# Seven block products instead of eight: Strassen's identity in the second feed-forward of a hybrid decoder layer

## The chip, the cores and the metric

The kernel runs on one core of a Trainium2 chip. The metric is the device time of one execution in microseconds (us). Engine names are TensorE (PE; PEld is its weight load), VectorE (DVE), ScalarE (ACT), GpSimd (POOL) and SyncE (SP), which issues nearly all DMAs.

## The reference

One decoder layer over 512 prompt tokens and 32 sample tokens (T = 544 columns), model width D = 1024, hidden width FF = 2816, all in float32. The layer is a feed-forward, a token mixer and a second feed-forward; each is followed by a layer norm.

```
yp = post_ln(yp, 0.5 * swiglu(yp, ffb_gate, ffb_up, ffb_down), ln3_g, ln3_b)
swiglu(x, w_gate, w_up, w_down) = (silu(x @ w_gate) * (x @ w_up)) @ w_down
post_ln(x, sub, g, b)           = layer_norm(ALPHA * x + sub, g, b)
```

The sample tokens take the same path. Only the second feed-forward (`ffb`) and the norm ahead of it are touched.

## The kernel before

Tokens lie transposed in SBUF: `x[128, 8, 544]`, eight chunks (KC) of 128 model rows. PSUM has eight banks of 512 float32 columns. Every float32 product is made of three products of rounded parts: an operand is split into a high part (ACT copies it to fp32r) and a low part (DVE subtracts the high part from the raw one), and TensorE adds high x high, high x low and low x high. A weight tile of 128 hidden columns is `graw` (raw, 128x1024), `ghi`, `glo`; one buffer of each for gate (0) and up (1).

`product` (L762) makes one gate or up tile: 8 chunks, 3 parts, 2 halves of 272 token columns, so 48 matmuls of 128x128 weights on 272 columns, into banks 0 and 1 (gate) or 2 and 3 (up). There are FT = 22 hidden tiles. They are taken in pairs; the down product of pair p-1 runs between the chunks of pair p:

- `tile(0)` and `tile(1)` (L930) make the first pair. `tile(0)` waits for the norm chunk by chunk (`norm_lo`); between the chunks of `tile(1)` stand five `rows_back` (L915), which transpose the normed tokens back for the residual.
- `window(i, par, p)` (L944) runs ten times. It makes pair p+1, and after every four chunks one `block` (L885) of pair p: 6 matmuls on 512 columns into bank 4, 5 or 6, which DVE adds to `yt` in `add_rows` (L1871). `few` (L904) does the same for the 32 sample tokens.
- A tail makes the down product of the last pair, and `rows_scale` and `rows_values` the last layer norm.

ACT per pair: silu of two gate tiles (`sg`, L1471), high parts of four weight tiles (L1392), of the hidden values (`hh`, L1467) and of the down weights (`ehi`, L1460). DVE per pair: the low parts of these (L1741, `hl` L1895, `elo` L1868), two gated products `ht` (L1890), eight `add_rows` (L1875) and one `add_few` (L1880). GpSimd does nothing in this stage. SP loads `graw` strips of 512 KB and `eraw` strips of 1 MB, each when its buffer is free.

Each engine runs its own program in a fixed order, and waits on semaphores that other engines count up.

The norm ahead (`norm_values(1)`, L1984, on DVE; `norm_scale(1)`, L1550, on ACT): DVE multiplies a chunk by the reciprocal deviation (L2014), ACT makes `xh` and `x` from it (L1565), DVE makes `xl` (L2010).

## Time and profile before

| | |
|---|---|
| median of 3 runs | 1372.5 us (1369.28 to 1373.71) |
| profiled execution, first to last instruction | 1372.2 us |
| PE, DVE, ACT, POOL busy | 94%, 55%, 31%, 18% of the span |
| mean granted TensorE clock | 0.978 |

The times of the three runs are given without saying which execution was profiled; its span of 1372.2 us lies among them, 0.3 us under their median, so the profiled execution can stand for the runs. What lies around the span is not recorded apart. A reader should ask first which engine is busy without a gap in the stage that changes, and only then what its instructions cost.

### The profile page before, as it was taken

The page shows a single profiled execution, that of the slowest core. Times are in us where ns is not written, and L with a number is a line of the kernel's source. Part 1 is how long each engine was busy: PE and PEld are TensorE (multiplying, and loading weights), DVE is VectorE, ACT ScalarE, POOL GpSimd, SP SyncE. Part 2 cuts the span into 40 slices and gives each one's busy share as a digit, 9 for nine tenths or more (in the row PEclk, how much of TensorE's full clock was granted, in tenths as well). Part 3 has the DMA queues.
Part 4 walks back from the last instruction along what each step waited for, and adds up shares of the span by engine and source line. Part 5 has one row for each costly group of instructions (what it writes and reads, how often), then busy time and mean ns, then how long its engine had stood idle before and what let it go on. Part 6 is the DMA issues. An engine that isn't in the chain of part 4 may idle for free.

```text
span 1372.2 us, 29896 instructions
## 1 busy us (share of the span) xinstructions
PE 1293.8 (94%) x11917; PEld 1180.1 (86%) x11917; DVE 756.9 (55%) x1215; ACT 431.1 (31%) x813; POOL 241.1 (18%) x237
## 2 busy tenths in 40 slices
PE   6999999999999888999989999896999999999996
PEld 5999999999999877999956666695999999999994
DVE  4676487467737765334446666647344444344446
ACT  4322222223312225222235555316321222122224
POOL 1352044114404405000135334000000000000000
PEclk9999999999999999999989999898999999999998
DMA  4887176246625522322278665132532333333211
GB/s 140 223 214 178 57 207 194 70 133 182 186 79 171 160 55 63 66 63 78 73 237 263 205 226 170 36 89 80 162 102 85 105 97 102 107 107 102 82 61 65
DMA packets 216192, 173.95 MB, mean 127 GB/s; under 512 B 22947, under 2 KB 206418, under 8 KB 215700
## 3 DMA queue, kind: packets, MB, share of 16 engines
q1 hardware_dynamic: 209940, 155.64, 38.6%
q0 software_dynamic: 6144, 16.79, 3.7%
q8 instruction: 78, 1.28, 0.4%
q14 instruction: 30, 0.25, 0.1%
HBM read 168.44 MB, written 8.10 MB: 129 GB/s over the span
## 4 chain that ended last, share of the span: by engine, by line
PE 78%; DVE 11%; ACT 4%; DMA 3%; issue 3%; SPq 1%; POOL 0%; DVEq 0%; ACTq 0%
PE ps L770 44%; PE ps L899 8%; PE ps L826 7%; PE ps L796 4%; DVE dlo L1746 3%; PE ps L1255 2%; DMA draw<-in_ffa_down_dram 2%; DVE glo L1741 1%; PE ps L1226 1%; PE ps L1291 1%; PE ps L1271 1%; PE ps L1340 1%; PE ps L1003 1%; PE ps L1213 1%; ACT xh L1565 1%
## 5 line engine op out<-in xcount | busy, mean ns | idle before, releaser
L770 PE MATMUL ps<-xh,ghi 128*128 128x272 f32 x1872 | 395.1, 293 | 16.9 <-DVE xl L2010 14.2
L770 PE MATMUL ps<-xl,ghi 128*128 128x272 f32 x1872 | 388.8, 289 | 0.0
L770 PE MATMUL ps<-xh,glo 128*128 128x272 f32 x1872 | 387.4, 288 | 0.0
L770 PEld LDWEIGHTS ps<-xh,ghi 128*128 128x128 f32 x1872 | 299.5, 189 | 33.8 <-issue 17.6
L770 PEld LDWEIGHTS ps<-xl,ghi 128*128 128x128 f32 x1872 | 296.2, 190 | 0.0
L770 PEld LDWEIGHTS ps<-xh,glo 128*128 128x128 f32 x1872 | 295.3, 190 | 0.0
L1741 DVE TENSOR_TENSOR glo<-graw,ghi 128x1024 fp32r<-128x1024 f32 x117 | 144.0, 1231 | 108.0 <-ACT ghi L1392 105.8
L726 POOL COPY perm<-landing 128x1024 f32<-128x1024 f32 x64 | 140.9, 2215 | 304.0 <-DMA landing<-in_cache_cmp_kv_dram 303.9
L1816 DVE SCALAR_TENSOR_TENSOR x<-ps,x 128x544 f32<-128x544 f32 x176 | 126.8, 720 | 104.7 <-PE ps L826 104.3
L1875 DVE SCALAR_TENSOR_TENSOR yt<-ps,yt 128x512 f32<-128x512 f32 x88 | 60.6, 691 | 156.6 <-PE ps L899 156.6
L1392 ACT ACTIVATE ghi<-graw 128x1024 fp32r<-128x1024 f32 x117 | 122.7, 1049 | 30.9 <-PE ps L770 20.9
L1398 ACT ACTIVATE dhi<-draw 128x128 fp32r<-128x128 f32 x176 | 53.2, 307 | 228.2 <-PE ps L826 207.9
L1746 DVE TENSOR_TENSOR dlo<-draw,dhi 128x128 fp32r<-128x128 f32 x176 | 108.1, 614 | 18.5 <-ACT dhi L1398 18.5
L399 POOL DMA_DIRECT2D page<-in_cache_sel_kv_dram x128 | 70.1, 549 | 227.4 <-issue 223.3
L826 PE MATMUL ps<-hh,dhi 128*128 128x272 f32 x352 | 77.2, 301 | 15.7 <-DVE dlo L1746 15.7
L826 PEld LDWEIGHTS ps<-hh,dhi 128*128 128x128 f32 x352 | 55.2, 190 | 21.7 <-DVE dlo L1746 21.1
L826 PE MATMUL ps<-hl,dhi 128*128 128x272 f32 x352 | 73.4, 290 | 0.0
L826 PE MATMUL ps<-hh,dlo 128*128 128x272 f32 x352 | 73.4, 290 | 0.0
L899 PE MATMUL ps<-ehi,hh 128*128 128x512 f32 x176 | 69.9, 397 | 1.7 <-DVE yt L1875 1.1
L899 PE MATMUL ps<-ehi,hl 128*128 128x512 f32 x176 | 69.4, 394 | 0.0
L899 PE MATMUL ps<-elo,hh 128*128 128x512 f32 x176 | 69.4, 394 | 0.0
L1467 ACT ACTIVATE hh<-ht 128x512 fp32r<-128x512 f32 x22 | 13.9, 632 | 159.3 <-DVE ht L1890 159.3
(344 smaller groups left out, 1492.5 us busy)
## 6 DMA issues: line engine op xcount, KB each, us to landing
landing<-in_cache_cmp_kv_dram SPq DMA_DIRECT2D x256, 128.0 KB, 2.5
page<-in_cache_sel_kv_dram SPq DMA_DIRECT2D x128, 128.0 KB, 4.9
page<-in_cache_sel_kv_dram POOLq DMA_DIRECT2D x128, 128.0 KB, 5.0
graw<-in_ffa_gate_dram SPq DMA_DIRECT2D x22, 512.0 KB, 4.9
graw<-in_ffa_up_dram SPq DMA_DIRECT2D x22, 512.0 KB, 4.1
draw<-in_ffa_down_dram SPq DMA_DIRECT2D x88, 128.0 KB, 2.8
graw<-in_w_in_dram SPq DMA_DIRECT2D x44, 256.0 KB, 3.3
graw<-in_ffb_gate_dram SPq DMA_DIRECT2D x22, 512.0 KB, 3.9
```

Of the source, the lines that this page charges most:

```text
L399: eng.dma_start(dst[:, DS(at + (j + k), 1), :], pool[0, DS(page, 1)].rearrange("o p c g d -> p o (c g d)")).then_inc(landed, 16)
L726: pool.tensor_copy(perm[:, :, :, at:at + QUAD].rearrange("p x d a -> p a x d"), landing[j % 2][:].rearrange("p a (x d) -> p a x d", d=HD)) ...
L770: last = nc.tensor.matmul(out[:, h, 0:HALF], a[:, k, :], b[:, k, h * HALF:(h + 1) * HALF], start=(k == 0 and a is hi and b is xhi), stop=( ...
L796: last = nc.tensor.matmul(ps[c * HD:(c + 1) * HD, bank + h, 0:G * PW], w1[rows, c, d, :], perm[rows, c * G:(c + 1) * G, d, :], start=(d == ...
L826: last = nc.tensor.matmul(ps[:, 4 + 2 * s + h, 0:HALF], a[:], b[:, h * HALF:(h + 1) * HALF], start=(a is dhi[s] and b is hh[par]), stop=(a ...
L899: last = nc.tensor.matmul(ps[:, 4 + k, :], x_part[:, rows], w_part[:, a, :], start=(a == 0 and x_part is h and w_part is ehi[n]), stop=(a ...
L1392: act.activation(ghi[s][:], graw[s][:], ACT.Copy).then_inc(w_hi[s], 1)
L1398: act.activation(dhi[s][:], draw[k % 2][:, s, :], ACT.Copy).then_inc(d_hi[s], 1)
L1741: dve.tensor_tensor(glo[s][:], graw[s][:], ghi[s][:].bitcast(F32), ALU.subtract).then_inc(w_lo[s], 1)
L1746: dve.tensor_tensor(dlo[s][:], draw[k % 2][:, s, :], dhi[s][:].bitcast(F32), ALU.subtract).then_inc(d_lo[s], 1)
L1816: dve.scalar_tensor_tensor(xt, ps[:, 4 + 2 * s:6 + 2 * s, 0:HALF], 0.5, xt, ALU.mult, ALU.add).then_inc(y_added[s], 1)
L1875: dve.scalar_tensor_tensor(part, ps[:, 4 + k, :], 0.5, part, ALU.mult, ALU.add).then_inc(y_added[0], 1)
```

## The change

The product of a pair of hidden tiles with the tokens is seen as a 2x2 by 2x2 block product: hidden tiles (2) by upper and lower half of the model width (2), times halves of the width by token halves, `near` (columns 0 to 271) and `far` (272 to 543). It is made from seven block products instead of eight (Winograd's form of Strassen's identity). A block product (`part`) has 4 chunks and 3 split parts, 12 matmuls of 272 columns. Seven left operands per pair and matrix: three blocks of the weights (A11, A12, A22) and four sums (S1 to S4), which GpSimd makes in `sums`. Seven right operands: three blocks of the tokens and four sums t1 to t4 (`tokens_of`), made once, after the norm.

- A group (w, s) is pair w, gate (s = 0) or up (s = 1). There are 11 x 2 groups. The operands of group g+1 are split while group g runs, into seven slots `slot_hi` and `slot_lo`.
- Four results come from seven products: ACT copies three partial sums out of PSUM (`snap`), DVE adds them to others (`quarter`), and further products add onto what stands in the bank.
- SP loads 256 hidden columns at once (1 MB, `pair_w`), and the loops are written out.
- The first two loads, and the stores of the key and value rows, are issued before `std_ready` is waited for.

```diff
+PARTS = 7
+WINDOWS = FT // 2
+A11, A12, S1, S2, S3, S4, A22 = range(PARTS)
+LOW_ORDER = (A11, A12, S1, S3, S2, S4, A22)
+LOW_AT = {k: n + 1 for n, k in enumerate(LOW_ORDER)}
...
+        t1 = (xh[:, upper, far], xl[:, upper, far], x_raw[:, upper, far])
+        tokens_of = ((xh[:, upper, near], xl[:, upper, near]), (xh[:, lower, near], xl[:, lower, near]), t1[0:2],
+                     (t2[0][:], t2[1][:]), (t3[0][:], t3[1][:]), (xh[:, lower, far], xl[:, lower, far]),
+                     (t4[0][:], t4[1][:]))
...
-                def gate_up(s, i):
-                    w = (gate, up)[s]
-                    col = value(i * 128)
-                    free_from(w_lo[s], i + (uses[s] + ONE))
-                    sp.dma_start(graw[s][:], w[0].rearrange("(k p) f -> p k f", p=128)[:, :, DS(col, 128)]
-                                 ).then_inc(dma_w[s], 16)
+                def group_load(s, p):
+                    g = 2 * (p - 1) + s
+                    if p:
+                        sp.wait_ge(*since("slot_low", PARTS * (g + 1)))
+                        sp.wait_ge(*since("s_made", 4 * (g + 1)))
+                    sp.dma_start(pair_w[s][:], (gate, up)[s][0].rearrange("(k p) f -> p k f", p=128)[:, :, p * 256:(p + 1) * 256]
+                                 ).then_inc(q[f"dma_wide{s}"], 16)
...
                 token_stores()
+                sp.wait_ge(stored, 16 * KV_STORES)
...
+            def sums(g):
+                p, s = divmod(g, 2)
+                a = lambda i, j: pair_w[s][:, (upper, lower)[j], i * 128:(i + 1) * 128]
+                at = lambda k: slot_raw[:, k]
+                def free(k):
+                    if g:
+                        pool.wait_ge(*since("part", PARTS * (g - 1) + k + 1))
+                pool.wait_ge(*since(f"dma_wide{s}", 16 * (p + 1)))
+                free(S1)
+                pool.tensor_tensor(at(S1), a(1, 0), a(1, 1), ALU.add).then_inc(q["s_made"], 1)
+                free(S2)
+                pool.wait_ge(*since("s_made", 4 * g + 1))
+                pool.tensor_tensor(at(S2), at(S1), a(0, 0), ALU.subtract).then_inc(q["s_made"], 1)
+                free(S3)
+                pool.tensor_tensor(at(S3), a(0, 0), a(1, 0), ALU.subtract).then_inc(q["s_made"], 1)
+                free(S4)
+                pool.wait_ge(*since("s_made", 4 * g + 2))
+                pool.tensor_tensor(at(S4), a(0, 1), at(S2), ALU.subtract).then_inc(q["s_made"], 1)
+            sums(0)
+            pool.wait_ge(normed, 2 * KC)
+            pool.tensor_tensor(t3[2][:], x[:, lower, far], x[:, upper, far], ALU.subtract
+                               ).then_inc(q["t3_raw"], 1)
+            for g in range(1, 2 * WINDOWS):
+                sums(g)
...
+                def part(g, k, bank, first):
+                    pe.wait_ge(*since("slot_low", PARTS * g + LOW_AT[k]))
+                    bh, bl = tokens_of[k]
+                    for c in range(K2):
+                        for a, b in ((slot_hi, bh), (slot_hi, bl), (slot_lo, bh)):
+                            last = nc.tensor.matmul(ps[:, bank, 0:HALF], a[:, k, c, :], b[:, c, :],
+                                                    start=(first and c == 0 and a is slot_hi and b is bh),
+                                                    stop=(c == K2 - 1 and a is slot_lo), skip_group_check=True)
+                    last.then_inc(q["part"], 1)
+                def group(w, s, between):
+                    g = 2 * w + s
+                    if w:
+                        pe.wait_ge(*since(("silu_done", "up_done")[s], 4 * w))
+                    if g == 0:
+                        pe.wait_ge(norm_lo, KC + K2)
+                    part(g, A11, s, True)
+                    if g:
+                        pe.wait_ge(*since("mixed_out", 3 * g - 2))
+                    else:
+                        pe.wait_ge(norm_lo, 2 * KC)
+                    part(g, A12, 2, True)
+                    between(0)
+                    if g:
+                        pe.wait_ge(*since("mixed_out", 3 * g))
+                    else:
+                        pe.wait_ge(*since("t_low", 1))
+                    part(g, S1, 3, True)
+                    pe.wait_ge(*since("snapped", 3 * g + 1))
+                    if g == 0:
+                        pe.wait_ge(*since("t_low", 2))
+                    part(g, S2, s, False)
+                    between(1)
+                    pe.wait_ge(*since("snapped", 3 * g + 3))
+                    if g == 0:
+                        pe.wait_ge(*since("t_low", 3))
+                    part(g, S3, s, False)
+                    between(2)
+                    part(g, S4, 3, False)
+                    pe.wait_ge(*since("mixed_out", 3 * g + 2))
+                    if g == 0:
+                        pe.wait_ge(*since("t_low", 4))
+                    part(g, A22, s, False)
+                    between(3)
...
+                    def blocks(n):
+                        def between(at):
+                            if n == 0 and at == 1:
+                                if p == 0:
+                                    pe.wait_ge(q["yt_begun"], QT + 1)
+                                few(p, par)
+                            for j in ((), (0,), (1,), (2, 3))[at]:
+                                block(p, par, QT * n + j, row_block)
+                        return between
+                    group(w, 0, blocks(0))
+                    group(w, 1, blocks(1))
...
+            def high(g, k):
+                p, s = divmod(g, 2)
+                if g:
+                    act.wait_ge(*since("part", PARTS * (g - 1) + k + 1))
+                if k in (A11, A12, A22):
+                    act.wait_ge(*since(f"dma_wide{s}", 16 * (p + 1)))
+                else:
+                    act.wait_ge(*since("s_made", 4 * g + k - S1 + 1))
+                act.activation(slot_hi[:, k], raw_block(s, k), ACT.Copy).then_inc(q["slot_high"], 1)
...
+                def silu(w, n, a, cols, src=None):
+                    dst = sg4[2 * (w % 2) + a][:, cols]
+                    if src is None:
+                        act.wait_ge(*since("mixed_out", 6 * w + n + 1))
+                    else:
+                        act.wait_ge(*since("part", PARTS * 2 * w + PARTS))
+                        if w >= 2:
+                            act.wait_ge(*since("h_low", 2 * (w - 1)))
+                    act.activation(dst, dst if src is None else src, ACT.Silu).then_inc(q["silu_done"], 1)
+                def snap(g, n):
+                    act.wait_ge(*since("part", PARTS * g + (1, 3, 4)[n]))
+                    if g:
+                        act.wait_ge(*since("mixed_out", 3 * (g - 1) + (1, 2, 3)[n]))
+                    act.activation((sum1, sum3, sum2)[n][:], ps[:, 3 if n == 1 else g % 2, 0:HALF], ACT.Copy
+                                   ).then_inc(q["snapped"], 1)
+                def group(w, s):
+                    g, p = 2 * w + s, w - 1
+                    more = g + 1 < 2 * WINDOWS
+                    if s == 0 and w:
+                        copy_h(p, 1)
+                    snap(g, 0)
+                        high(g + 1, A11)
+                    if s == 0 and w:
+                        split_e(1, p, p == 0)
+                    if s == 1:
+                        split_e(0, w, w == 0)
+                    if more:
+                        high(g + 1, A12)
+                    if s == 0:
+                        silu(w, 0, 0, near)
+                    if w == 0:
+                        rows_begun(0 if s == 0 else QT)
+                    snap(g, 1)
+                    snap(g, 2)
+                    if more:
+                        high(g + 1, S1)
+                        high(g + 1, S2)
+                    if g == 0:
+                        rows_begun(1)
+                    if s == 0:
+                        silu(w, 1, 1, far)
+                    if g == 0:
+                        rows_begun(2)
+                    if more:
+                        high(g + 1, S3)
+                    if s == 0:
+                        silu(w, 2, 0, far)
+                    if more:
+                        high(g + 1, S4)
+                    if s == 0:
+                        silu(w, 3, 1, near, ps[:, 0, 0:HALF])
+                    else:
+                        copy_h(w, 0)
+                    if g == 0:
+                        rows_begun(3)
+                    if more:
+                        high(g + 1, A22)
...
+                    for k in (A11, A12, S1, S2):
+                        high(0, k)
...
+            def slot_lower(g, k):
+                n = LOW_AT[k] - 1
+                dve.wait_ge(*since("slot_high", PARTS * g + k + 1))
+                if g:
+                    dve.wait_ge(*since("part", PARTS * (g - 1) + k + 1))
+                if k in (S1, S2):
+                    dve.wait_ge(*since("s_made", 4 * g + (2, 4)[k - S1]))
+                dve.tensor_tensor(slot_lo[:, k], raw_block(g % 2, k), slot_hi[:, k].bitcast(F32), ALU.subtract
+                                  ).then_inc(q["slot_low"], 1)
...
+                def quarter(w, s, n, a, cols, out_part, first, second):
+                    g = 2 * w + s
+                    dst = (sg4, ht4)[s][slot_of(w, a)][:, cols]
+                    dve.wait_ge(*since("part", PARTS * g + out_part))
+                    dve.wait_ge(*since("snapped", 3 * g + n + 1))
+                    dve.tensor_tensor(dst, first, second, ALU.add).then_inc(q["mixed_out"], 1)
+                    if s == 1:
+                        dve.wait_ge(*since("silu_done", 4 * w + 4))
+                        dve.wait_ge(*since("mixed_out", 3 * g + n + 1))
+                        last = dve.tensor_tensor(dst, dst, sg4[slot_of(w, a)][:, cols], ALU.mult)
+                        last.then_inc(q["up_done"], 1)
+                        if n == 2:
+                            dve.wait_ge(*since("up_done", 4 * w + 3))
+                            dve.engine_nop().then_inc(q["h_ready"], 1)
...
+                    if s == 0 and w >= 1:
+                        low(p, 1)
                     if more:
-                        split_w(0, i + (uses[0] + 2))
-                    add_rows(p, 6, row_block)
-                    split_e(0, p + 1)
-                split_w(0, uses[0] + 1)
+                        slot_lower(g + 1, A11)
+                    quarter(w, s, 0, 0, near, 2, bank(2), sum1[:])
+                    if more:
+                        slot_lower(g + 1, A12)
+                    if s == 0 and w:
+                        split_e(1, p)
+                    if s == 1:
+                        split_e(0, w)
+                    if w:
+                        if p == 0 and s == 0:
+                            dve.wait_ge(q["yt_begun"], QT + 1)
+                        add_rows(p, 4 * s, row_block)
+                        if s == 0:
+                            add_few(p)
+                    if more:
+                        slot_lower(g + 1, S1)
+                    quarter(w, s, 1, 1, far, 5, bank(s), sum3[:])
+                    if w:
+                        add_rows(p, 4 * s + 1, row_block)
+                    if more:
+                        slot_lower(g + 1, S3)
+                    quarter(w, s, 2, 0, far, 6, bank(3), sum2[:])
+                    if more:
+                        slot_lower(g + 1, S2)
+                    if s == 1:
+                        dve.wait_ge(*since("part", PARTS * g + PARTS))
+                        dve.tensor_tensor(ht4[slot_of(w, 1)][:, near], bank(s), sg4[slot_of(w, 1)][:, near], ALU.mult
+                                          ).then_inc(q["up_done"], 1)
+                        dve.wait_ge(*since("up_done", 4 * w + 4))
+                        dve.engine_nop().then_inc(q["h_ready"], 1)
+                        low(w, 0)
+                        add_rows(p, 4 * s + 2, row_block)
+                    if more:
+                        slot_lower(g + 1, S4)
+                        slot_lower(g + 1, A22)
...
                 low(KC - 2)
                 low(KC - 1)
+                if n == 1:
+                    def token_low(k, dst, src, high_part):
+                        dve.wait_ge(*since("t_high", k + 1))
+                        dve.tensor_tensor(dst, src, high_part.bitcast(F32), ALU.subtract
+                                          ).then_inc(q["t_low"], 1)
+                    raw1, raw2, raw4 = t1[2], t2[2][:], t4[2][:]
+                    dve.tensor_tensor(raw1, x[:, upper, far], x[:, upper, near], ALU.subtract).then_inc(q["t_raw"], 1)
+                    dve.wait_ge(*since("t_raw", 1))
+                    dve.tensor_tensor(raw2, x[:, lower, far], raw1, ALU.subtract).then_inc(q["t_raw"], 1)
+                    token_low(0, t1[1], raw1, t1[0])
+                    slot_lower(0, S3)
+                    dve.wait_ge(*since("t_raw", 2))
+                    dve.tensor_tensor(raw4, x[:, lower, near], raw2, ALU.subtract).then_inc(q["t_raw"], 1)
+                    slot_lower(0, S2)
+                    token_low(1, t2[1][:], t2[2][:], t2[0][:])
+                    token_low(2, t3[1][:], t3[2][:], t3[0][:])
+                    slot_lower(0, S4)
+                    token_low(3, t4[1][:], t4[2][:], t4[0][:])
+                    slot_lower(0, A22)
             ffa_values()
             norm_values(0)
```

## Rows read from the trace of the kernel before

**Rows 1.** The page: engines (busy us, share, instructions); a group (busy us, mean ns).

```profile
PE 1293.8 (94%) x11917; PEld 1180.1 (86%) x11917; DVE 756.9 (55%) x1215; ACT 431.1 (31%) x813; POOL 241.1 (18%) x237
...
L770 PEld LDWEIGHTS ps<-xh,ghi 128*128 128x128 f32 x1872 | 299.5, 189 | 33.8 <-issue 17.6
```

**Rows 2.** Windows: stretch, length, busy us of each engine, PEclk, DMA share, GB/s.

```profile
1032.00:1064.00 32.00, 32.00 (x228) 29.41 (x227) 13.59 (x17) 7.44 (x10) 0.00 (x0) 1.00 0.28 84
...
1192.00:1224.00 32.00, 32.00 (x229) 29.41 (x228) 14.69 (x18) 6.11 (x8) 0.00 (x0) 1.00 0.35 110
```

**Rows 3.** The chain that ended last, 1188 to 1230 us: start, us, what.

```profile
1191.25 3.00 PE ps L770 x24
1194.25 1.40 PE ps L899 x6
...
1227.64 2.39 PE ps L770 x19
```

**Rows 4.** Timeline of PE, eight transposes with eight different weights between products.

```profile
968.81 1.03 PE L923 MATMUL ps<-ident,x 128*128 128x128 f32 x8
969.60 0.50 PE L770 MATMUL ps<-xh,ghi 128*128 128x272 f32 x2
```

**Rows 5.** Groups by form, 960 to 1372 us: busy us, mean ns of one, idle before.

```profile
L1875 DVE SCALAR_TENSOR_TENSOR yt<-ps,yt 128x512 f32<-128x512 f32 x88 | 60.6, 691 | 156.6 <-PE ps L899 156.6
L1741 DVE TENSOR_TENSOR glo<-graw,ghi 128x1024 fp32r<-128x1024 f32 x42 | 51.2, 1218 | 9.0 <-ACT ghi L1392 9.0
...
L1895 DVE TENSOR_TENSOR hl<-ht,hh 128x512 fp32r<-128x512 f32 x22 | 15.0, 683 | 1.4 <-ACT hh L1467 1.4
L1467 ACT ACTIVATE hh<-ht 128x512 fp32r<-128x512 f32 x22 | 13.9, 632 | 159.3 <-DVE ht L1890 159.3
...
L1880 DVE SCALAR_TENSOR_TENSOR ys<-ps,ys 128x256 f32<-128x256 f32 x11 | 4.7, 424 | 17.7 <-PE ps L911 17.7
...
L1487 ACT ACTIVATE ys<-ps 128x256 f32<-128x256 f32 x1 | 0.4, 384 | 1.1 <-PE ps L926 1.1
```

**Rows 6.** Timeline of DVE at the end: two instructions in a row.

```profile
1357.73 1.28 DVE L1875 SCALAR_TENSOR_TENSOR yt<-ps,yt 128x512 f32<-128x512 f32 x2
```

**Rows 7.** Groups of POOL, whole span.

```profile
L726 POOL COPY perm<-landing 128x1024 f32<-128x1024 f32 x64 | 140.9, 2215 | 304.0 <-DMA landing<-in_cache_cmp_kv_dram 303.9
...
L754 POOL TENSOR_TENSOR xl<-yconv,xh 128x544 fp32r<-128x544 f32 x4 | 5.4, 1344 | 0.3
```

**Rows 8.** Timeline, POOL and DVE, 67 to 76 us, while both work.

```profile
67.04 4.03 POOL L726 COPY perm<-landing 128x1024 f32<-128x1024 f32 x2 [8.72 <-DMA landing<-in_cache_cmp_kv_dram]
73.73 3.18 POOL L726 COPY perm<-landing 128x1024 f32<-128x1024 f32 x1 [2.66 <-DMA landing<-in_cache_cmp_kv_dram]
...
69.02 0.71 DVE L1816 SCALAR_TENSOR_TENSOR x<-ps,x 128x544 f32<-128x544 f32 x1
69.66 1.38 DVE L1746 TENSOR_TENSOR dlo<-draw,dhi 128x128 fp32r<-128x128 f32 x1
...
73.75 1.22 DVE L1741 TENSOR_TENSOR glo<-graw,ghi 128x1024 fp32r<-128x1024 f32 x1
```

**Rows 9.** Timeline, DVE in the norm ahead of the stage.

```profile
937.03 1.29 DVE L1995 TENSOR_TENSOR sq<-sq 128x1088 f32<-128x1088 f32 x1 [1.18 <-ACT sq L1555]
...
957.27 0.72 DVE L2010 TENSOR_TENSOR xl<-x,xh 128x544 fp32r<-128x544 f32 x1 [0.74 <-ACT x L1565]
```

**Rows 10.** Timeline, PE at the start of the stage.

```profile
947.89 0.79 PE L770 MATMUL ps<-xh,ghi 128*128 128x272 f32 x2 [5.75 <-DVE xl L2010]
948.48 0.66 PE L770 MATMUL ps<-xl,ghi 128*128 128x272 f32 x2
948.94 0.65 PE L770 MATMUL ps<-xh,glo 128*128 128x272 f32 x2
...
981.25 0.41 PE L770 MATMUL ps<-xh,ghi 128*128 128x272 f32 x2
```

**Rows 11.** Timeline, PE at the end of the last window.

```profile
1345.14 0.40 PE L899 MATMUL ps<-elo,hh 128*128 128x512 f32 x1
1345.47 1.07 PE L911 MATMUL ps<-eraw,ht 128*32 128x256 f32 x16
1346.97 0.47 PE L899 MATMUL ps<-ehi,hh 128*128 128x512 f32 x1 [0.43 <-DVE hl L1895]
```

**Rows 12.** DMA issues: KB each, median us from issue to landing.

```profile
eraw<-in_ffb_down_dram SPq DMA_DIRECT2D x11, 1024.0 KB, 4.9
w<-in_cmp_w_dram SPq DMA_DIRECT2D x4, 1024.0 KB, 8.3
```

More of the change, by code:

```diff
@@ L238, in trunk, with raw_under, split_pair @@
         rows = ExitStack()
-        sb("under_rows", [128, 12000], F32, rows)
+        def raw_under(name, shape):
+            with ExitStack() as over:
+                return sb(name, shape, F32, over)
+        def split_pair(name):
+            upper_part = sb(f"{name}_0", [128, KC // 2, HALF], F32R, rows)
+            raw_part = raw_under(f"{name}_raw", [128, KC // 2, HALF])
+            return upper_part, sb(f"{name}_1", [128, KC // 2, HALF], F32R, rows), raw_part
+        t2 = split_pair("t2")
+        t3 = split_pair("t3")
+        sb("under_groups", [128, T], F32, rows)
+        sum3 = sb("sum3", [128, HALF], F32, rows)
+        sb("before_groups", [128, 896 - T - HALF], F32, rows)
+        pair_w = [sb(f"pair_w{n}", [128, KC, 256], F32, rows) for n in range(2)]
+        slot_hi = sb("slot_hi", [128, 7, KC // 2, 128], F32R, rows)
+        slot_raw = raw_under("slot_raw", [128, 7, KC // 2, 128])
+        slot_lo = sb("slot_lo", [128, 7, KC // 2, 128], F32R, rows)
+        t4 = split_pair("t4")
+        ln_rows = sb("ln_rows", [128, 2, D], F32, rows)
+        ln_s = sb("ln_s", [128, 2, 256], F32, rows)
+        eraw = sb("eraw", [128, 2, D], F32, rows)
         over = ExitStack()
@@ L889, in block @@
                     if j == 0:
-                        pe.wait_ge(hl_ready, p * 2 + (FT + 2 + ONE))
+                        pe.wait_ge(*since("h_low", p * 2 + 2))
                     if order is row_block:
@@ L944, in window @@
-                def window(i, par, p):
-                    def first(c):
-                        if c % 4 == 0:
-                            if c == 4:
-                                pe.wait_ge(q["yt_begun"], QT + 1)
-                            block(p, par, c // 4 - 1, row_block)
-                        if c == 6:
-                            few(p, par)
-                    def second(c):
-                        if c % 4 == 0:
-                            block(p, par, QT + c // 4 - 1, row_block)
-                    tile(i, None, first)
-                    tile(i + 1, None, second)
@@ L961, in ffb_products @@
-                pe.wait_ge(std_ready, 4)
-                tile(0, (norm_lo, KC))
-                turns = {2: 0, 4: 1, 8: 2, 12: 3, 14: 4}
-                tile(1, None, lambda c: rows_back(turns[c]) if c in turns else None)
-                with pe.Fori(0, FT // 4) as i:
-                    for par in range(2):
-                        window(i * 4 + (2 + 2 * par), par, i * 2 + par)
+                def part(g, k, bank, first):
[7 more added lines that the diff above has]
+                    last.then_inc(q["part"], 1)
@@ new lines, in first_gate, with first_up @@
+                def first_gate(at):
+                    rows_back(at)
+                def first_up(at):
+                    if at == 0:
+                        rows_back(QT)
+                group(0, 0, first_gate)
+                group(0, 1, first_up)
+                for w in range(1, WINDOWS):
+                    p, par = w - 1, (w - 1) % 2
+                    def blocks(n):
[9 more added lines that the diff above has]
+                    group(w, 1, blocks(1))
@@ L1525, in rows_scale @@
+                for w in range(WINDOWS):
+                    for s in range(2):
+                        group(w, s)
+                copy_h(WINDOWS - 1, 1)
+                split_e(1, WINDOWS - 1)
             def rows_scale():
@@ L1570, in norm_scale, with token_high @@
                     affine(x[:, k, :], x[:, k, :], k).then_inc(normed, 1)
+                if n == 1:
+                    def token_high(k, dst, src):
+                        if k == 2:
+                            act.wait_ge(*since("t3_raw", 1))
+                        else:
+                            act.wait_ge(*since("t_raw", (1, 2, 0, 3)[k]))
+                        act.activation(dst, src, ACT.Copy).then_inc(q["t_high"], 1)
+                    token_high(0, t1[0], t1[2])
+                    token_high(1, t2[0][:], t2[2][:])
+                    high(0, S3)
+                    token_high(2, t3[0][:], t3[2][:])
+                    high(0, S4)
+                    token_high(3, t4[0][:], t4[2][:])
+                    high(0, A22)
             ffa_gates()
@@ L2009, in low @@
                     dve.wait_ge(normed, KC * n + k + 1)
-                    dve.tensor_tensor(xl[:, k, :], x[:, k, :], xh[:, k, :].bitcast(F32), ALU.subtract
+                    cols = near if n == 1 and k < K2 else slice(0, T)
+                    dve.tensor_tensor(xl[:, k, cols], x[:, k, cols], xh[:, k, cols].bitcast(F32), ALU.subtract
                                       ).then_inc(norm_lo, 1)
```

226 lines of the change are left out of this document (82 added, 144 removed).

## The prediction, made before the changed kernel ran

> **What bounds the kernel now.** I read the page first [rows 1]: TensorE is busy 94% of the span. That is a mean over stages, so I then read the second feed-forward in stretches of 32 us: TensorE is busy in all 32, at full clock (2.4 GHz), VectorE in 14, ScalarE in 6 to 7, GpSimd in none [rows 2]. The chain of work that ended last says the same in order of time: 24 products of 3.00 us, 6 down products of 1.40 us, and again, with nothing between [rows 3]. So here a matmul taken away is time taken away, as long as no other engine comes to hold TensorE up. The same piece stands at 1191.25 and at 1227.64 us: a window lasts 36.39 us. The ten windows begin at 981.25 [rows 10] and end at 1345.14 + 0.23 = 1345.37 (the last down matmul starts at 1345.14 [rows 11]; six take 1.40, so one 0.23), and 1372.2 - 1345.4 = 26.8 us of tail follow.
>
> **TensorE's own work.** A pair had 2 x 2 x 48 = 192 gate and up matmuls and gets 2 x 7 x 12 = 168. At 3.00 us for 24, one costs 0.125 us, so a pair loses 3.0 us and a window becomes 33.4 us; eleven pairs save 33. Before, each load of weights served one of two halves, and now each load brings other weights. Bounded from both sides: the profile has a weight load for every matmul already (11917 of each [rows 1]), and eight transposes with eight different weights start within 0.79 us, 0.10 us apiece [rows 4], under 0.125. So I take 0.125, the nearest row. The other end is 0.19, a weight load's own duration [rows 1], if each load had to end before its matmul and began after the last: windows of 44 us. Already 0.132 would undo the gain, so this is a rival below.
>
> The Trainium skill (TensorE: Matmul & The Clock Gate, "Back-to-back issue gap") gives a sustained 81 ns for 128 columns and 131 ns for 512. An estimate between these is 105 ns for 272 columns, by which 264 matmuls would save 28 us and not 33; the trace has 125 ns and about 232 ns, so the sum goes by the trace.
>
> **VectorE's work in a window.** A following instruction costs less than its own duration: two of 691 ns take 1.28 us [rows 5, 6], so 0.60 to 0.64 us apiece; I take 0.60 for 512 columns, 1.14 for 1024 (1218 less 0.08) and 0.36 for 272 (424 less 0.08 for 256). Low parts of slots 14 x 0.60 = 8.4 (before 4 x 1.14 = 4.6); down weights 2 x 1.14 = 2.3; additions of rows 8 x 0.60 and 0.35 = 5.2; hidden low parts 1.2; quarters 6 additions and 4 products, 10 x 0.36 = 3.6, and some 0.5 of waits for itself: 21.2 us of 33.4. ScalarE: 14 slots, 6 snaps, 4 silus, 2 hidden and 2 down copies, at 0.55, 0.33, 0.33, 0.55 and 0.97 us from its rows [rows 5], are 14 us. Both fit.
>
> **GpSimd's work.** Eight sums of 128x512. The nearest row is a two-operand instruction on 544 columns, 1344 ns [rows 7]: 1.27 us apiece, 10.1 per window. Below it can hardly be less, since the row has contiguous operands and these are strided; from above, the copy of 1024 strided columns takes 2.1 us undisturbed (two in 4.03 [rows 8]), and if two inputs of 512 cost as much as one of 1024, a sum takes 2.1. I take 1.27, the same operation.
>
> **They hold each other up.** While GpSimd copies (67.04 to 71.07), a subtraction of 128x128 on VectorE starting at 69.66 takes 1.38 us, that is until 71.04, where GpSimd ends; the same instruction takes 0.3 elsewhere. The other way round, the copy from 73.73 takes 3.18 us where VectorE subtracts 1024 columns at 73.75. But the addition from PSUM at 69.02 keeps its 0.71 [rows 8]. So VectorE's instructions with both inputs in SBUF and GpSimd's sums exclude one another: 8.4 + 2.3 + 1.2 + 1.1 (three products) = 13.0 and 10.1 us, 23.1 of 33.4. Even if VectorE stood still during every sum it would be 31.4. It fits, with 2 us to spare in the worst case.
>
> The Trainium skill (SBUF — State Buffer, "Who interferes with whom") calls this an exclusive lock held for the whole instruction. The rule alone, which lets either side wait fully, makes 31.4 us in a window the ceiling; the walk below has less. The trace agrees on the exclusion and on the PSUM exception.
>
> **Order within a group.** TensorE waits where a sum is copied out: `S3` waits for the snap after `S2`. Between them stands one down block, 1.40 us; ScalarE needs about 0.2 to notice, 0.35 to copy: 0.8 spare. `A22` waits for the quarter after `S3`: between them a block and `S4`, 2.9 us, and VectorE may be behind a slot's low part which waits for GpSimd's second sum. Walking both groups with these prices, VectorE ends the gate group 1 us late and the up group 2.4 us late, and catches up in the 4 us before the next down block; the quarter is ready 1.7 us early at its tightest. Loads: 1 MB lands in 5 to 8 us [rows 12] and has some 9 in hand. So I cost the steady window at 33.4 and no stall.
>
> **The start is dearer.** Before, tile 0 ran chunk by chunk behind the norm from 947.89, and the windows began at 981.25 [rows 10]. Now the third product waits for token sums. VectorE finishes the norm at 957.27 + 0.72 = 958.0 [rows 9], 0.3 later for two more copies on ScalarE. GpSimd's token sum (1088 columns, 2 x 1.34 = 2.7 us) gets in first: 961. Then VectorE has 3 token subtractions and 4 token low parts, 1.21 apiece (1.29 less 0.08 [rows 9]), four slot low parts, 0.7 of waits, and two sums of GpSimd (2.5) that hold it: about 14 us, 975. Only then come one slot's low part and the first quarter (976), on which ScalarE's silu, one copy of rows back, and the two snaps wait (978.5); `S3` waits for these. What is left of the first pair on TensorE: three products of group 0 and seven of group 1 at 1.5, transposes of 2.3, one uncovered snap of 0.8: 18.1, 996.6. TensorE will have stood still for over 5 us again (its second product and transposes end near 973), and after such a pause its matmuls cost 0.23 instead of 0.125 for some 5 us [rows 10]: 2.3 more, 999. That is 17.7 us later than 981.25. Bounds: 989 if GpSimd never holds VectorE and the clock stays up; 1006 if each hold is twice as long.
>
> The tail is unchanged: the hidden low part is ready about as late after the last block as it was (a wait of 0.43 [rows 11]).
>
> **Sum.** 999 + 10 x 33.4 + 0.3 + 26.8 = 1360.1 us for the span; with 0.3 for what the median lies above it [1372.5 against 1372.2], 1360.4. That is 12 us, 0.9%, faster: 30 saved in the windows, 18 lost at the start. Its own range, by the bounds of the start and half a microsecond per window, is 1350 to 1368.
>
> **The rivals.**
>
> *The start is hidden.* If the silu and snaps don't stand behind the token work, the start costs nothing more: 1372.5 - 33 = 1339, up to 1350 when half of it shows. Against it: the instruction order on VectorE puts all token low parts before the first quarter. 0.06.
>
> *Stalls in the window.* Each group has two waits with 0.8 and 1.7 us to spare; if a group loses 0.6 us, the ten windows are 34.6 us each and the gain is gone: 1372. Half to double of that is 1366 to 1384. For it: a 1.27 us sum is longer than the spare. Against it: in the walk ScalarE needs nothing from VectorE between `S1` and the snap in the up group. 0.15.
>
> *GpSimd bounds the stage (slower).* If a sum takes 2.1 us and VectorE is held for all of each, a window is 21.2 + 8 x 2.1 = 38.0 us: 999 + 380 + 27 = 1406. It decides from (34.6 - 21.2) / 8 = 1.68 us per sum. For it: strided inputs, and VectorE's queue in fixed order, which makes a hold of one instruction a delay of all. Against it: the 1344 ns row, and that additions from PSUM aren't held. 0.13.
>
> *Other weights cost.* At 0.14 us per matmul instead of 0.125 a window is 168 x 0.14 + 12.3 (down products and sample tokens: 36.4 less 24.1) = 35.8 us, the end 999 + 358 + 27 = 1384; at 0.132 nothing is gained. For it: this is the one thing that the trace of before shows only for 128 columns. Against it: there it is 0.10 us [rows 4]. 0.06.
>
> **Chances.** My forecast has 0.60, the four rivals 0.06, 0.15, 0.13 and 0.06. A measurement of this kernel can tell about 0.3% (4 us) from no change. Faster: 0.60 + 0.06 + 0.05 of the stalls + 0.01 of the weights = 0.72. Slower: 0.13 + 0.05 + 0.03 = 0.21. Within: the other 0.07. The range leaves out most of the first rival and of the third: 1346 to 1384.
>
> **What would show it.** Right: the chain in the windows alternates 12 products of 1.5 us with blocks, 33.4 us between equal pieces, TensorE at 32 of 32; POOL's sums near 1.3 us; the first window begins near 999 after a pause of some microseconds before the first `S3`. Wrong: idle time of PE before a part, released by ACT `sum` (snap) or DVE (quarter, slot low part); POOL sums over 1.7 us; VectorE's slot low parts at well over 0.68 us in the mean; products more than 0.125 apart within a part.

## The result, and the profile after

The changed kernel takes 1359.55 us (median of 5, 1355.53 to 1360.82), the kernel before, run beside it, 1369.28 (1364.48 to 1373.71): a ratio of 0.9912 with a 95% interval of 0.9886 to 0.9939, so 0.9% faster. The prediction's sum was 1360.4, its range 1346 to 1384. The profiled execution took 1359.71 us, its span is 1358.1.

The page's first part answers to [rows 1]: TensorE has 264 matmuls fewer and 29 us less to do, VectorE, ScalarE and GpSimd have more.

```profile
PE 1264.8 (93%) x11653; PEld 1150.5 (85%) x11653; DVE 864.7 (64%) x1420; ACT 508.2 (37%) x1015; POOL 375.0 (28%) x326
```

Windows of 33 us in the second feed-forward (columns as in [rows 2]):

```profile
1136.00:1169.00 33.00, 33.00 (x230) 30.11 (x229) 22.76 (x38) 14.73 (x28) 11.85 (x9) 1.00 0.32 108
1237.00:1270.00 33.00, 33.00 (x230) 30.11 (x229) 22.76 (x38) 14.97 (x28) 11.88 (x9) 1.00 0.33 108
```

TensorE is still busy in all of the stretch at full clock. VectorE went from 14 to 23 us, ScalarE from 7 to 15, GpSimd from nothing to 12, and none of it reaches TensorE. The chain that ended last agrees (start, us, what; with [rows 3]):

```profile
1114.62 6.03 PE ps L1024 x48
1124.95 3.03 PE ps L1024 x24
1127.98 2.80 PE ps L987 x12
1130.78 6.02 PE ps L1024 x48
1137.81 1.58 PE ps L987 x6
...
1148.13 6.03 PE ps L1024 x48
```

1148.13 - 1114.62 = 33.51 us is a window, where 36.39 was. 48 matmuls take 6.03: 0.126 us apiece, though the weights now change ahead of two matmuls in three (`part` uses a high weight block for two matmuls in a row, a low one for one), where they changed ahead of one in three. The sample tokens' row comes once per pair and is the easiest clock for windows (PE's timeline):

```profile
1001.34 1.07 PE L999 MATMUL ps<-eraw,ht 128*32 128x256 f32 x16
...
1136.73 1.07 PE L999 MATMUL ps<-eraw,ht 128*32 128x256 f32 x16
```

It stands at 1001.34, 1036.21, 1069.72 and so on to 1304.27: a first window of 34.87 and then 33.51 or 33.50 each time. The first is 1.36 us longer, nearly all of it one wait for the snap of a bank on ScalarE, which no later window has:

```profile
1005.10 0.52 PE L1024 MATMUL ps<-t,slot_hi 128*128 128x272 f32 x2 [1.10 <-ACT sum L1626]
```

ScalarE's snap is queued behind a silu that waits for VectorE's first quarter (L2083), and that quarter is late because two of VectorE's low parts, 0.68 us when free, met GpSimd's sums for the next group:

```profile
1000.17 1.79 DVE L2073 TENSOR_TENSOR hl<-ht,hh 128x512 fp32r<-128x512 f32 x1
1001.88 1.77 DVE L2062 TENSOR_TENSOR slot_lo<-pair_w,slot_hi 128x512 fp32r<-128x512 f32 x1
1003.58 0.43 DVE L2083 TENSOR_TENSOR sg<-ps,sum 128x272 f32<-128x272 f32 x1
...
1000.04 1.37 POOL L829 TENSOR_TENSOR slot_raw<-pair_w 128x512 f32<-128x512 f32 x1 [4.35 <-PE ps L1024]
1001.56 1.55 POOL L832 TENSOR_TENSOR slot_raw<-slot_raw,pair_w 128x512 f32<-128x512 f32 x1
```

**The start.** PE's timeline again: the norm's last product, the waits, and the first row of the second pair.

```profile
931.50 8.78 PE L1124 MATMUL ps<-sq,mean_w 128*128 128x272 f32 x24 [2.06 <-ACT sq L1709]
950.05 0.59 PE L1024 MATMUL ps<-xh,slot_hi 128*128 128x272 f32 x1 [9.77 <-DVE xl L2220]
958.50 0.59 PE L1024 MATMUL ps<-xh,slot_hi 128*128 128x272 f32 x1 [5.35 <-DVE xl L2220]
967.54 0.49 PE L1024 MATMUL ps<-t,slot_hi 128*128 128x272 f32 x2 [3.55 <-DVE t L2232]
975.21 0.82 PE L1024 MATMUL ps<-t,slot_hi 128*128 128x272 f32 x2 [3.56 <-ACT sum L1626]
990.58 0.51 PE L1024 MATMUL ps<-t,slot_hi 128*128 128x272 f32 x2 [0.49 <-ACT sum L1626]
...
995.20 0.29 PE L1024 MATMUL ps<-xh,slot_hi 128*128 128x272 f32 x1
```

Where one long wait of 5.75 us stood [rows 10], TensorE now stands still four times, 22.2 us together. VectorE's and GpSimd's timelines show what is done meanwhile:

```profile
955.41 3.03 DVE L2220 TENSOR_TENSOR xl<-x,xh 128x544 fp32r<-128x544 f32 x1 [0.74 <-ACT x L1721]
958.37 1.28 DVE L2236 TENSOR_TENSOR x_raw<-x 128x1088 f32<-128x1088 f32 x1
...
970.37 1.75 DVE L2062 TENSOR_TENSOR slot_lo<-pair_w,slot_hi 128x512 fp32r<-128x512 f32 x1
...
972.78 0.43 DVE L2083 TENSOR_TENSOR sg<-ps,sum 128x272 f32<-128x272 f32 x1
...
955.39 2.47 POOL L841 TENSOR_TENSOR t_raw<-x 128x1088 f32<-128x1088 f32 x1 [34.14 <-ACT x L1721]
...
970.03 1.54 POOL L832 TENSOR_TENSOR slot_raw<-slot_raw,pair_w 128x512 f32<-128x512 f32 x1 [4.34 <-PE ps L1024]
```

The norm's last low part takes 3.03 us instead of 0.72: it starts 0.02 us after GpSimd's token sum of 2.47, waits for it, and then runs. From 958.37 to 972.78 lie 14.4 us of token and slot parts, two of them held as well, and only then comes the first quarter, on which silu, copy, snaps and the product at 975.21 hang in a row. The clock was down before that last pause: in the product behind the pause of 3.55 us the matmuls stand 0.23 us apart from 968.4 on. Behind the pause of 3.56 the granted clock is 0.57 (window 975 to 979) and they stand 0.23 apart again; from 980 it is 1.00, and they stand 0.125 apart.

**The account.** The second pair's window opened at 981.25 [rows 10] and now does at 995.20; but the norm's row at 931.50 stood at 933.46 before, 2.0 us later. That row stands up to 7.5 us apart between traces of the kernels below, so these 2.0 us aren't put down to the change. From that row the start costs 63.7 instead of 47.8 us: 15.9 lost. Ten windows took 364.1 us and take 336.5 (to 1331.43 + 0.23): 27.7 won. The tail is 0.4 shorter. -2.0 + 15.9 - 27.7 - 0.4 = -14.2, and the spans differ by 14.1. Without the norm's row the change is worth 12.2 us in this pair of traces; the medians differ by 9.7.

### The profile page after: what moved, and what is told of

Read it like the earlier page. It is cut to its first block, busy times and chain, and to the rows that moved or that the text cites. A ratio compares the mean times of both kernels' runs of the same rounds, so it can differ in the third digit from the quotient of the medians.

```text
span 1358.1 us, 30053 instructions
## 1 busy us (share of the span) xinstructions
PE 1264.8 (93%) x11653; PEld 1150.5 (85%) x11653; DVE 864.7 (64%) x1420; ACT 508.2 (37%) x1015; POOL 375.0 (28%) x326
## 4 chain that ended last, share of the span: by engine, by line
PE 77%; DVE 12%; ACT 4%; issue 3%; DMA 2%; POOL 0%; SPq 0%; DVEq 0%; ACTq 0%; POOLq 0%
PE ps L859 26%; PE ps L1024 16%; PE ps L987 8%; PE ps L915 7%; PE ps L885 4%; DVE dlo L1917 3%; PE ps L1376 2%; DVE glo L1912 1%; DMA draw<-in_ffa_down_dram 1%; PE ps L1412 1%; PE ps L1392 1%; PE ps L1347 1%; DVE x L1987 1%; PE ps L1334 1%; PE ps L1124 1%
## 5 line engine op out<-in xcount | busy, mean ns | idle before, releaser
L859 PE MATMUL ps<-xh,ghi 128*128 128x272 f32 x1168 | 246.6, 293 | 10.4 <-DVE xl L2220 7.8
L859 PE MATMUL ps<-xl,ghi 128*128 128x272 f32 x1168 | 242.8, 289 | 0.0
L859 PE MATMUL ps<-xh,glo 128*128 128x272 f32 x1168 | 242.1, 289 | 0.0
L859 PEld LDWEIGHTS ps<-xh,ghi 128*128 128x128 f32 x1168 | 184.2, 190 | 14.5 <-issue 7.1
L859 PEld LDWEIGHTS ps<-xl,ghi 128*128 128x128 f32 x1168 | 184.9, 190 | 0.0
L859 PEld LDWEIGHTS ps<-xh,glo 128*128 128x128 f32 x1168 | 184.4, 190 | 0.0
L469 POOL DMA_DIRECT2D page<-in_cache_sel_kv_dram x128 | 69.8, 546 | 228.8 <-issue 224.5
L1024 PE MATMUL ps<-xh,slot_hi 128*128 128x272 f32 x352 | 103.0, 293 | 15.1 <-DVE xl L2220 15.1
L1024 PE MATMUL ps<-t,slot_hi 128*128 128x272 f32 x528 | 104.4, 292 | 8.7 <-ACT sum L1626 5.1
L1024 PE MATMUL ps<-xh,slot_lo 128*128 128x272 f32 x352 | 102.9, 292 | 0.0
L1024 PE MATMUL ps<-xl,slot_hi 128*128 128x272 f32 x352 | 102.2, 290 | 0.0
L1024 PEld LDWEIGHTS ps<-xh,slot_hi 128*128 128x128 f32 x352 | 67.3, 191 | 17.9 <-DVE xl L2220 15.9
```

The costliest lines, as they stand in the source:

```text
L469: eng.dma_start(dst[:, DS(at + (j + k), 1), :], pool[0, DS(page, 1)].rearrange("o p c g d -> p o (c g d)")).then_inc(landed, 16)
L859: last = nc.tensor.matmul(out[:, h, 0:HALF], a[:, k, :], b[:, k, h * HALF:(h + 1) * HALF], start=(k == 0 and a is hi and b is xhi), stop=( ...
L1024: last = nc.tensor.matmul(ps[:, bank, 0:HALF], a[:, k, c, :], b[:, c, :], start=(first and c == 0 and a is slot_hi and b is bh), stop=(c = ...
```

## The experiments

All are the changed kernel with one edit, except where said; ratios are to the kernel before on the same chip. Four of them (token sums left out, all sums twice, sums on VectorE, eight products) were measured beside runs of the kernel before with a median of 1369.22 us, the other four beside runs with 1370.86. Code lines are shortened. "The start" of a run is the time from the norm's row to the first sample row: 69.8 us in the changed kernel (1001.34 - 931.50).

**Token sums left out.** All seven products read parts of the normed tokens that are there anyway, no token sum is made, and the output is not the reference's. The norm's low parts of the upper chunks are made for both token halves again, which adds a little to VectorE's work.

```
+b11, b21, b12, b22 = [(xh[:, k, c], xl[:, k, c]) for c in (near, far) for k in (upper, lower)]
+tokens_of = (b11, b21, b12, b12, b12, b22, b21)
-token_low(0, t1[1], raw1, t1[0])    # and the others, their highs and raw sums
```

> The four sums of token blocks and their splits are left out (the products read plain token blocks instead, so the second feed-forward's result is another); all else stays, the seven products, the weight sums on GpSimd, the order of work. Theory A (the windows are bound by TensorE at 33.5 us, and the late start comes from the token work that VectorE must end before the first quarter): the windows stay at 33.5 us, the first window begins some 10 to 12 us earlier than in the changed kernel (3 subtractions and 4 low parts at 1.21 us and GpSimd's 2.5 us are gone), and the time falls to about 1348 us, ratio to the kernel before about 0.984. Rival B (the start is late because the first pair itself, with ScalarE's silu, copies of rows back and snaps in one queue, is slow whatever the tokens do): the first window begins at most 4 us earlier, the time stays above 1355.

Measured: 1347.60 us (1341.36 to 1349.21), ratio 0.9834 [0.9797, 0.9871]. PE's timeline has these waits left, and its sample row already at 991.66:

```profile
933.56 7.28 PE L1112 MATMUL ps<-sq,mean_w 128*128 128x272 f32 x24 [2.06 <-ACT sq L1697]
952.29 0.59 PE L1020 MATMUL ps<-xh,slot_hi 128*128 128x272 f32 x1 [11.45 <-DVE xl L2204]
958.15 0.59 PE L1020 MATMUL ps<-xh,slot_hi 128*128 128x272 f32 x1 [2.77 <-DVE xl L2204]
980.90 0.39 PE L1020 MATMUL ps<-xh,slot_hi 128*128 128x272 f32 x1 [0.49 <-ACT sum L1614]
...
991.66 1.07 PE L995 MATMUL ps<-eraw,ht 128*32 128x256 f32 x16
```

The start is 58.1 us, 11.7 less than with the token sums. The windows are 33.41 us instead of 33.51, and the first still has a wait of 1.08. So the token sums cost 11.7 us at the start and 0.10 in each window: without them a piece of 24 matmuls in the chain takes 3.00 us instead of 3.03. Why products with a token sum are this much slower, no run shows.

**All weight sums twice.** Each of GpSimd's four sums of a group is preceded by the same sum into a dead buffer.

```
+pool.tensor_tensor(kc_all, a(1, 0), a(1, 1), ALU.add)
 pool.tensor_tensor(at(S1), a(1, 0), a(1, 1), ALU.add)
```

> Each of GpSimd's weight sums is computed twice, first into a spare place and then into its slot (some 2.6 us instead of 1.3 per sum). The prediction's third rival says that a window is 21.2 + 8 x d us if VectorE is held for all of each sum of d us: with d = 2.6 that is 42 us, 10 windows 85 us longer, a time of about 1445 us. Theory A (VectorE is held only where an instruction with both inputs in SBUF meets a sum, and GpSimd's own 21 us of 33.5 fit): TensorE now waits for low parts of slots in some groups, since the second and fourth sums end over 2 us later; windows of 34 to 37 us, time 1362 to 1395.

Measured: 1389.94 us (1387.91 to 1394.41), ratio 1.0163 [1.0128, 1.0199]; windows 36.05, and a start of 78.8 us, 8.9 more than in the changed kernel. The chain, for the first time, leaves TensorE:

```profile
1098.60 2.33 POOL kc_all L832
1100.92 1.26 POOL slot_raw L833
...
1102.31 1.31 POOL kc_all L838
1103.61 1.26 POOL slot_raw L839
...
1106.61 0.44 DVE ht L2096
1107.05 0.04 issue
1107.09 1.78 PE ps L1037 x12
```

VectorE's low part of `S1` waits for GpSimd's second sum, which still reads the raw `S1` that the low part is written over; the quarter is queued behind it; TensorE's product of `A22` waits for the quarter. That happens once per group. GpSimd is busy 22.7 us in 33 (mean of two stretches), so its own time doesn't bound the stage, and VectorE isn't held for each sum: the doubled load costs 2.5 us a window and not 8.6 (the rival's 42). Of the 30.7 us between the spans, about 22 come from the windows and 8.9 from the start.

**Half of the weight sums twice.** The same for `S3` and `S4` only: 12 sums a pair.

> Only two of the four weight sums of a group are made twice (into a buffer that nobody reads), so 12 sums a pair instead of 8, or 16 in the run where all were made twice, whose windows were 36.05 us. Theory A (a sum costs nothing until its lateness reaches the quarter behind it in VectorE's queue; some 1 us is spare): half the load leaves windows at 33.5 to 34.2, 1359 to 1366 us. Rival (each sum takes its price from VectorE through the exclusion, in proportion): half of the 2.5 us, so 34.8, 1372 to 1375.

Measured: 1358.97 us (1356.67 to 1363.95), ratio 0.9924 [0.9890, 0.9959]; windows 33.51. In a stretch of 33 us:

```profile
1136.00:1169.00 33.00, 33.00 (x230) 30.26 (x229) 25.53 (x38) 14.71 (x28) 17.52 (x12) 1.00 0.31 108
```

GpSimd is 5.7 us busier than in the changed kernel, VectorE shows 2.8 us more (its holds), and the window doesn't move by 0.01. So a sum has no price in proportion. It doesn't follow that the number of sums decides: the two doubled here are the third and the fourth, and the wait of the run above comes from the second. `S1` and `S2` alone weren't doubled in any run. At the start it isn't free either: 71.6 us, 1.8 more than in the changed kernel, and the first window is 0.17 longer.

**Weight sums on VectorE.** GpSimd makes those of the first gate group only; VectorE makes the others ahead of the low parts that need them.

```
+sum_on_dve(g + 1, S1)
+sum_on_dve(g + 1, S2)
 slot_lower(g + 1, S1)
```

> The weight sums of all groups but the first are made by VectorE, between its other instructions, and GpSimd makes none in this stage. Theory A (both places are off the path): 8 x 0.6 = 4.8 us more work of VectorE in a window of 33.5, of which 26 to 27 busy, no holds; windows stay at 33.5 us and the time within 0.3% of the changed kernel, 1356 to 1363 us. Rival D (VectorE's fixed order makes each added instruction a delay of the quarter, which TensorE waits for before A22, and of the snaps at the start): windows of 34.5 us or more, time over 1368 us. Rival E (GpSimd's holds cost the changed kernel something in the windows): the time falls below 1355 us.

Measured: 1357.05 us (1350.07 to 1360.64), ratio 0.9903 [0.9868, 0.9937]; windows 33.51 again:

```profile
1136.00:1169.00 33.00, 33.00 (x232) 30.29 (x224) 26.39 (x45) 14.57 (x27) 0.00 (x0) 1.00 0.31 106
```

VectorE carries all of it with 6.6 us to spare. GpSimd's help isn't needed, and from the second window on it isn't in the way. Before that it is: without its sums the start is 68.8 us (1001.44 - 932.66), 1.1 less, and the first window is 33.51, 1.4 less, with no wait for a snap. Rival E had this right in kind, 2.4 us in all, though the time stays above its 1355.

**Eight products.** Of a group's seven products one (`A12`) is made twice; everything else stays.

```
+part(g, A12, 2, True, False)
 part(g, A12, 2, True)
```

> The product of A12 is made twice in each group, the second over the first, so TensorE makes eight block products of 12 matmuls as the kernel before did; sums, splits, snaps and quarters stay. Theory A (windows bound by TensorE alone): each of 22 groups is 1.5 us longer, windows 33.5 + 3.0 = 36.5 us, and the time is 1359.5 + 33 = 1392 us at most, 1388 where the first pair's product falls into a pause; ratio to the kernel before about 1.015. Rival C (the window's length is set by waits between engines): an added product fills pauses and the time grows by under 20 us.

Measured: 1391.97 us (1389.16 to 1394.94), ratio 1.0167 [1.0138, 1.0196]; windows 36.53, near the 36.39 of the kernel before, and a start of 72.9 us, 3.1 more than with seven products. The eighth product costs 36.53 - 33.51 = 3.02 us a pair, the forecast 3.0. It also gives what the change would be without the identity: all of the cost at the start, no gain in the windows, 1.7% slower than before.

**The first pair plain.** This is the version that the experiments pointed to. The first pair is made by eight products as before, chunk by chunk behind the norm, its half tiles in the slots of the sums; the token sums are made while it runs, and the seven products begin with the second pair.

```
+for i in range(4):
+    first_tile(i, {2: 0, 4: 1, 8: 2, 12: 3, 14: 4})    # i = gate, up, gate, up; rows back as before
-group(0, 0, first_gate)
-group(0, 1, first_up)
 for w in range(1, WINDOWS):
```

> The first tile pair is made by the eight plain products again, chunk by chunk behind the norm, and the sums of the tokens are made while it runs; the seven products begin with the second pair. Theory A (the start is dear because VectorE's and ScalarE's token sums stand between the norm and the first products, 12 us by the run without them): the PE row that opens the second pair's window comes 13 to 18 us earlier against the norm's mean products than in the changed kernel, one pair costs 3.0 us more TensorE time, which the gain already counts; windows stay at 33.5; 1342 to 1347 us. Rival (the start is bound by the norm itself and a slow clock after it, and the sums only fill that time): no more than 4 us, 1355 to 1360.

Measured: 1343.39 us (1341.59 to 1351.25), ratio 0.9812 [0.9776, 0.9848]. PE's timeline:

```profile
928.82 8.78 PE L1146 MATMUL ps<-sq,mean_w 128*128 128x272 f32 x24 [2.06 <-ACT sq L1766]
943.35 0.79 PE L1082 MATMUL ps<-xh,slot_hi 128*128 128x272 f32 x2 [5.75 <-DVE xl L2301]
...
955.85 0.82 PE L1082 MATMUL ps<-xh,slot_hi 128*128 128x272 f32 x2 [2.79 <-DVE xl L2301]
...
980.38 0.29 PE L1035 MATMUL ps<-xh,slot_hi 128*128 128x272 f32 x1
...
986.51 1.07 PE L1010 MATMUL ps<-eraw,ht 128*32 128x256 f32 x16
1020.02 1.07 PE L1010 MATMUL ps<-eraw,ht 128*32 128x256 f32 x16
```

From the norm's row to the second pair are 51.6 us, against 63.7 in the changed kernel and 47.8 before; and the first window is 33.51, without the wait of 1.10. The row is 12.1 us earlier, a little less than the 13 to 18 of theory A, and 13.5 with the wait; the time is where that theory put it. The norm's row itself is 2.7 earlier here, and together they are the 16.2 by which the spans differ (1358.1 and 1341.9). What is left of the start, 3.8 us more than before, is one wait of 2.79, in which the norm's last low part (3.06 us from 952.73) again stands behind GpSimd's token sum (2.51 from 952.71), and the slow clock after it.

**The first pair plain, sums on VectorE.** Both edits together.

> The first pair plain, and from the second pair's up group on the weight sums on VectorE in place of GpSimd. Theory A (VectorE has the room in a window, and no sum there is late): windows 33.5 us, within 3 us of the kernel with the first pair plain, 1340 to 1348. Rival (the sums on GpSimd are what keeps the windows at 33.5, and without them VectorE's queue delays a quarter somewhere): windows above 34, 1350 or more.

Measured: 1345.47 us (1339.51 to 1349.86), ratio 0.9811 [0.9775, 0.9848]; windows 33.51. Its norm stood 3.0 us later than in the run above, its span is 3.0 longer. There is nothing to choose between the two.

**The changed kernel again**, unedited, beside the runs with 1370.86.

> The changed kernel itself on the same chip, as the measure for the others: 1357 to 1361 us by every theory.

Measured: 1357.51 us (1354.32 to 1363.52), ratio 0.9910 [0.9874, 0.9946]. The plain first pair is 14.1 us under it.

## Why the prediction was right

**TensorE's price.** 0.125 us per matmul was taken over, on the ground that transposes with eight different weights cost less, and is 0.126 in the chain; the eighth product, put back, costs 3.02 us a pair. The rival "other weights cost" is out for this order of work. It was put too strongly, though: not every load brings other weights, since the high block of a chunk serves two matmuls in a row, so new weights for each matmul of 272 columns were not measured. The prediction's estimate of 105 ns for 272 columns is not on a straight line between the 81 and 131 ns that it starts from, which gives 100; the chain's 126 ns is above both, and the sum rightly went by the trace.

**The window.** 33.4 was forecast, 33.51 came. VectorE was put at 21.2 us of 33.4 and shows 22.8 in 33 (its holds are counted as busy), ScalarE 14 and 14.9, GpSimd 10.1 and 11.9. The difference of GpSimd is one sum per group. Its own timeline, with a row of VectorE:

```profile
1101.94 2.26 POOL L829 TENSOR_TENSOR slot_raw<-pair_w 128x512 f32<-128x512 f32 x1 [7.62 <-PE ps L1024]
1104.34 1.29 POOL L832 TENSOR_TENSOR slot_raw<-slot_raw,pair_w 128x512 f32<-128x512 f32 x1
...
1101.84 1.22 DVE L2039 TENSOR_TENSOR elo<-eraw,ehi 128x1024 fp32r<-128x1024 f32 x1
```

A free sum is 1.29 us (forecast 1.27). The first of a group starts 0.10 us after VectorE's split of down weights, waits the 1.12 us that this still runs, and shows 2.26. So strided operands didn't cost more, and the 2.1 of the upper bound is met only as a hold.

**No stall.** Right for nine windows of ten; the first has one of 1.10 us, not forecast, and the run with the sums on VectorE shows that GpSimd's sums cause it. The walk's spare time was real: in a later up group the quarter ends at 1124.20 and the product `A22` that needs it starts at 1126.29, 2.1 us after it, where the walk had 1.7 at its tightest. The run with all sums twice shows the wait that the prediction named as the sign of a failure (a quarter behind a slot's low part), once the second sum comes late enough. The rival "stalls in the window" is out at this load.

**GpSimd bounds the stage.** Its formula, VectorE's work and in addition every sum in full, was wrong as a mechanism: it would make 21.2 + 16 x 1.29 = 41.8 us of the doubled sums, and 36.05 came. VectorE waits for TensorE in part of each group, and sums that fall there cost it nothing.

**The start.** 17.7 us was forecast, 15.9 came from the norm's row. In the terms of the walk, with 2.0 us taken off for the earlier norm: end of the norm's low parts 959.0 forecast, 958.4 measured; first quarter 974 and 972.8; the product `S3` 976.5 and 975.2; windows 997.0 and 995.2. The mechanism and its order are as written, and the run without token sums and the one with the first pair plain take 11.7 and 12.1 us of it away. The remainder of the walk after `S3` (20.5 us forecast, slow clock included) took 20.0. In one point the walk was off: a pause of over 5 us before `S3` and some 5 us of slow matmuls were forecast, 3.56 and about 3.3 came.

**What made up the total.** The windows gave 2.4 us less than the 30 forecast (0.1 per window and the longer first one), the start took 1.8 less than 17.7, the tail 0.4 less, and 2.0 came from ahead of the stage. The 0.3 us that stand in the sum ahead of the tail have no source, and no run shows them. That 1360.4 came within 1 us of the median is partly luck, since these cancel. The difference was forecast less closely: 12 us from a median of 1372.5, and 9.7 came, because the kernel before, run beside the changed one, had a median of 1369.28.

## What to carry to other kernels

Where TensorE is busy for the whole of a stage, an identity that trades products for sums pays in full as long as the other engines have room, and their room is to be read as lateness at the instruction that TensorE waits for and not as busy share: doubling GpSimd's third and fourth sums cost the windows nothing, doubling all four cost 2.5 us a window. Look for the price of such a change at its first turn, where little yet covers the sums: here 15.9 us were lost there against 27.7 won in ten windows, and doing the first turn the old way won 13.5 back. Compare traces from a common row just ahead of the change, since what lies before it moves by itself (the norm's row stood between 928.7 and 936.2 us in nine traces of kernels that are the same up to there).

## What the runs showed of the hardware

- VectorE and GpSimd exclude each other by whole instructions, in both directions, as in [rows 8]: a VectorE instruction of 0.72 us shows 3.03 when it starts just behind a GpSimd sum of 2.47, a GpSimd sum of 1.29 shows 2.26 when it starts just behind one of VectorE's. The Trainium skill (SBUF — State Buffer, "Who interferes with whom") calls it an exclusive lock; the trace agrees. Not expected was how little it costs: 17.5 us of GpSimd beside 25.5 of VectorE in 33 left TensorE without a wait. Where VectorE has no slack it does cost: two such holds ahead of one quarter are behind the 1.10 us wait of the first window.
- TensorE's granted clock fell to 1.2 GHz after quite short pauses: in the kernel with the first pair plain, 2.79 us of standing still behind chunks with small gaps were followed by 3 us at a mean granted clock of 0.53 and matmuls 0.23 us apart; from 960 it was 1.00.
- With weights that change ahead of two matmuls of 272 columns in three, a matmul came to 0.126 us, against 0.125 where they changed ahead of one in three. The profile shows a weight load for every matmul in both kernels, and 0.19 us for each; both can hold only if the loads, as the profile records them, overlap with matmuls and with each other.
